# One core, a two-part network: transposes inside a chunked scan by VectorE, the scan's walk cut in thirds, and bias products taken out of two projections

## What is computed

```python
z = jax.nn.gelu(h @ w_in + b_in, approximate=False)
u, v = jnp.split(z, 2, axis=-1)
v = layernorm(v, ln_g, ln_b, LN_EPS)
v = v.reshape(bsz, n // CHUNK, CHUNK, GMLP_GROUPS, GMLP_GROUP_CH)
v = jnp.einsum('gpq,bcqgd->bcpgd', w_s, v) + b_s.T[:, :, None]
return (u * v.reshape(bsz, n, GMLP_WIDTH)) @ w_out + b_out
```

## Time and profile before

| | us |
|---|---|
| median of 3 runs | 5302.05 (5282.6 to 5308.4) |
| the profiled execution | 5314.02 |
| its span, first to last instruction | 5312.1 |
| TensorE busy in it | 3985.8 |
| stage gmi, its v half | about 2071 to 2261 |
| stage gmo | about 2330 to 2486 |
| the scan, heads 0 to 15 and the last walk | about 3690 to 4485 |

### The profile page before, as it was taken

One profiled execution on the slowest core, in us unless ns is written; L12 is line 12 of the kernel. 1 busy time (PEld: TensorE's weight loads), 2 busy tenths in 40 slices (PEclk: granted clock), 3 DMA queues, 4 the chain that ended last, 5 costly groups with the idle time before them and its releaser, 6 DMA issues. The chain is left out here.

```text
span 5312.1 us, 89186 instructions
## 1 busy us (share of the span) xinstructions
PE 3985.8 (75%) x34888; PEld 2795.1 (53%) x34888; DVE 2115.7 (40%) x4471; ACT 1349.1 (25%) x2720; POOL 1215.1 (23%) x899
## 2 busy tenths in 40 slices
PE   7755898767599869977487773876999996347784
PEld 6434676544477657664322221753888886322221
DVE  3433764435476433253200004642666663510002
ACT  2222331222333132110111111113555543111111
POOL 4101343310143424342100001421333332300000
PEclk9756899876899989888698897988999997759887
DMA  3211453222255311113399994344221222349997
GB/s 117 71 46 56 166 174 100 76 69 55 70 183 174 90 57 57 36 61 138 123 421 422 422 422 189 111 129 145 52 57 44 52 57 63 118 178 418 420 420 284
DMA packets 349502, 842.25 MB, mean 159 GB/s; under 512 B 126089, under 2 KB 191453, under 8 KB 289406
## 3 DMA queue, kind: packets, MB, share of 16 engines
q1 hardware_dynamic: 340630, 808.97, 42.4%
q0 software_dynamic: 8560, 28.85, 1.5%
HBM read 744.79 MB, written 92.93 MB: 158 GB/s over the span
## 5 line engine op out<-in xcount | busy, mean ns | idle before, releaser
L1123 DVE SCALAR_TENSOR_TENSOR f_ada<-first_hT,condition,f_ada 128x256 f32 (+1 forms) x672 | 287.1, 499 | 0.0
L2566 DVE TENSOR_TENSOR scan_R<-scan_R,scan_bank 128x256 f32<-128x256 f32 x240 | 100.9, 420 | 231.4 <-PE scan_bank L2589 229.8
L1885 PE MATMUL moe0e_p_g<-moe_ring,moe0e_xT 128*64 128x512 f32 x608 | 174.3, 653 | 17.9 <-issue 9.2
L342 POOL TENSOR_TENSOR gmi_w_lo<-gmi_w,gmi_w_hi 128x512 fp32r<-128x512 f32 x64 | 122.2, 1910 | 239.1 <-ACT gmi_w_hi L361 239.1
L2340 POOL TENSOR_TENSOR scan_off<-scan_pairs,scan_join 128x256 f32<-128x256 f32 x240 | 174.3, 765 | 0.0
L1885 PE MATMUL moe0e_p_u<-moe_ring,moe0e_xT 128*64 128x512 f32 x608 | 167.7, 631 | 0.0
L2589 PE MATMUL scan_bank<-scan_R,scan_Z 64*64 64x64 f32 x3840 | 155.1, 219 | 10.3 <-DVE scan_R L2566 9.7
L2589 PE MATMUL scan_bank<-scan_T,scan_off 64*64 64x64 f32 x3840 | 157.2, 220 | 5.6 <-issue 0.6
L1885 PE MATMUL moe1e_p_g<-moe_ring,moe1e_xT 128*64 128x512 f32 x512 | 148.2, 660 | 15.1 <-issue 8.3
L342 POOL TENSOR_TENSOR p_w_lo<-p_w,p_w_hi 128x512 fp32r<-128x512 f32 (+3 forms) x88 | 112.8, 1283 | 176.9 <-ACT p_w_hi L361 176.9
L1904 PE MATMUL moe0e_p_y<-moe_ring,moe0e_gatedT 128*64 128x512 f32 x608 | 142.8, 624 | 13.0 <-ACT moe0e_gatedT L1929 13.0
(11 more groups left out here) (707 smaller groups left out, 10659.3 us busy)
## 6 DMA issues: line engine op xcount, KB each, us to landing
moe_ring<-in_moe_w_gu_dram SPq DMA_DIRECT2D x280, 1024.0 KB, 21.9
moe_ring<-in_moe_w_down_dram SPq DMA_DIRECT2D x140, 1024.0 KB, 22.5
first_hT<-in_ada_w_dram SPq DMA_DIRECT2D x48, 1024.0 KB, 7.3
f0u_w<-in_ffn_w_gate_up_dram SPq DMA_DIRECT2D x22, 1024.0 KB, 4.9
f1u_w<-in_ffn_w_gate_up_dram SPq DMA_DIRECT2D x22, 1024.0 KB, 4.9
gmi_w<-in_ga_w_in_dram SPq DMA_DIRECT2D x64, 256.0 KB, 2.7
p_w<-in_ab_w_in_dram SPq DMA_DIRECT2D x48, 256.0 KB, 2.7
f0d_w<-in_ffn_w_down_dram SPq DMA_DIRECT2D x44, 256.0 KB, 2.7
```

The lines of the kernel that those rows point to most:

```text
L342: nc.gpsimd.tensor_tensor(w_lo[t % 2][:, 0:width], w[t % RAW][:, 0:width], w_hi[t % 2][:, 0:width], ALU.subtract).then_inc(w_lo_made, 1)
L1123: ins = nc.vector.scalar_tensor_tensor(out=dst, in0=src, scalar=cond[:, k, which:which + 1], in1=dst, op0=ALU.mult, op1=ALU.add)
L1885: mm = nc.tensor.matmul(p[r, :], xT[:, kd, r], ring[:, s, half, k, g * HID:(g + 1) * HID], start=(kd == 0), stop=(kd == KD - 1), skip_grou ...
L2566: V.tensor_tensor(R[u][:, g4, :], R[u][:, g4, :], quad(zr_bank), ALU.add).then_inc(s["zr_added"], 1)
```

## The change

In the scan:

- T comes from VectorE: after each addition into R (and after the identity is added) VectorE waits for its own write and transposes the 128x256 tile in 32x32 blocks. The twelve grown turns and the three root turns by TensorE go, and with them ScalarE's 15 copies of T. After the last level, which joins the 32-wide blocks, T is not made.
- The walk's steps 3 to 11 are cut in thirds: each slot has two thirds, one before its Z times R product and one after it, so that they fill slots 0 to 13. The product of r with the state moves from `walk_state` to `walk_solve`.
- See and the copy of y move from VectorE to ScalarE, and t1 (one 128x768 instruction per head) too.
- The bonus sums move from the start of the front part to behind `walk_state` of step 2. The sums of squares move from slot 2 to slot 5.
- b and k are turned into one bank per group and copied by three ScalarE instructions of 128x512 instead of six of 128x256. Z times R has two banks in turn, so its wait is for the addition two slots back.
- SyncE loads sg on its own, earlier; the other six transfers stay at the start of a head.

In the gated MLP:

- The bias products go. For v, VectorE adds a bias row, which is now loaded on all 128 partitions, and ScalarE does the Gelu in place, SBUF to SBUF, in steps 2 and 3 of the next job.
- For the output, GpSimd makes bias times gate (two instructions of 128x1024, in steps 1 and 2) and adds it to the six x tiles (128x1024 each, steps 3 to 8) behind its own subtractions.

```diff
@@ project_split
-                        mm = nc.tensor.matmul(view(g), l_lo[:, a:a + aw], r_hi[:, b0:b0 + bw], start=False, stop=(last and bias is None))
-                        if last and bias is not None:
-                            mm = nc.tensor.matmul(view(g), const["ones"][0:1, 0:aw], bias, start=False, stop=True)
+                        mm = nc.tensor.matmul(view(g), l_lo[:, a:a + aw], r_hi[:, b0:b0 + bw], start=False, stop=last)
...
+                    if aside:
+                        aside(pool, t)
...
+                    if jobs[c].get("post"):
+                        nc.scalar.wait_ge(dve_done, nth[g])
+                        jobs[c]["post"](groups[g][1]).then_inc(posted, 1)
@@ gmlp
-            brow = mem2.enter_context(nc.sbuf_tensor("gm_brow", [1, W_GMLP], F32))
+            brow = mem2.enter_context(nc.sbuf_tensor("gm_brow", [P, W_GMLP], F32))
...
-                    return engine.activation(v[:, j, c * BANK:(c + 1) * BANK], ps, ACT.Gelu)
+                    cols = slice(c * BANK, (c + 1) * BANK)
+                    return engine.tensor_tensor(v[:, j, cols], ps, brow[:, cols], ALU.add)
...
+                    return nc.scalar.activation(v[:, j, cols], v[:, j, cols], ACT.Gelu)
...
+            if 1 <= t <= 2:
+                nc.gpsimd.tensor_tensor(gated_bias[t - 1][:], brow[:], gates[t - 1][:], ALU.mult).then_inc(bias_gated, 1)
+            if 3 <= t < 3 + NA:
+                j = t - 3
+                pool.wait_ge(bias_gated, 2)
+                nc.gpsimd.tensor_tensor(tiles[j], tiles[j], gated_bias[j >= NT][:], ALU.add).then_inc(bias_added, 1)
@@ rwkv_scan
-    WALK_GROWTH = {n: NG + n for n in range(STEPS - NG)}
+    WALK_PARTS = [(what, j) for j in range(NG, STEPS) for what in range(3)] + [(0, STEPS)]
...
@@ rwkv_scan, ScalarE
+                def walk_x(w, j):
+                    if j > CSTEPS:
+                        n = j - 1 - CSTEPS
+                        act.wait_ge(s["y_ready"], w * lat + n + 1)
...
+                        A(yo[:, n, :], y_psum, ACT.Copy).then_inc(s["y_copied"], 1)
+                    if j < STEPS:
+                        act.wait_ge(s["x_ready"], w * STEPS + j + 1)
+                        A(X[:], x_psum, ACT.Copy).then_inc(s["x_copied"], 1)
+                    if 1 <= j < STEPS - 1:
+                        act.wait_ge(s["sm_ready"], w * STEPS + j + 1)
+                        A(See[:], Sm[:], ACT.Identity, scale=ee[w % 2][:, j:j + 1]).then_inc(s["step_made"], 1)
...
+                    if slot == 2:
+                        if h:
+                            act.wait_ge(s["km_made"], h)
+                        A(t1[:], aa[:], ACT.Identity, scale=cols(h, 1), bias=oneminus[:, h:h + 1]).then_inc(s["t1_made"], 1)
...
@@ rwkv_scan, VectorE
+                    def turn(g):
+                        g4 = slice(4 * g, 4 * g + 4)
+                        V.transpose(T[:, g4, :].rearrange("p c t -> p (c t)"), R[u][:, g4, :].rearrange("p c t -> p (c t)")).then_inc(s["t_made"], 1)
...
+                        walk_part(2 * n)
                         dve.wait_ge(s["zr_ready"], h * NZ + n + 1)
-                        V.tensor_tensor(R[u][:, g4, :], R[u][:, g4, :], quad(zr_bank), ALU.add).then_inc(s["zr_added"], 1)
-                        if walk is not None and n in WALK_GROWTH:
-                            walk_step(walk, WALK_GROWTH[n])
+                        V.tensor_tensor(R[u][:, g4, :], R[u][:, g4, :], quad(zr_bank[n % 2]), ALU.add).then_inc(s["zr_added"], 1)
+                        if l < LEVELS - 1:
+                            dve.wait_ge(s["zr_added"], h * NZ + n + 1)
+                            turn(g)
+                        walk_part(2 * n + 1)
...
@@ rwkv_scan, TensorE
                     for n in range(NZ):
...
-                        part(walk_state, j)
-                        if 1 <= n <= NZ - NG:
-                            turn_grown(n - 1)
-                        part(walk_solve, j)
+                        walk_part(2 * n)
                         pe.wait_ge(s["z_copied"], h * NZ + n + 1)
-                        if n >= 1:
-                            pe.wait_ge(s["zr_added"], h * NZ + n)
+                        if n >= 2:
+                            pe.wait_ge(s["zr_added"], h * NZ + n - 1)
                         for q in range(4):
-                            mm = mmul(zr_bank[:, q * CH:(q + 1) * CH], Z[n % 2][:, q, :], R[u][:, 4 * g + q, :])
+                            mm = mmul(zr_bank[n % 2][:, q * CH:(q + 1) * CH], Z[n % 2][:, q, :], R[u][:, 4 * g + q, :])
                         mm.then_inc(s["zr_ready"], 1)
-                        part(walk_share, j)
+                        walk_part(2 * n + 1)
```

More of the change, by code:

```diff
@@ L363, in _ @@
                         ends("act", act, nc.scalar, chain, act_done, c - 1, k)
+                    if c and 2 <= k < 4:
+                        posts(c - 1, k - 2)
                 for half in range(2):
                     ends("act", act, nc.scalar, chain, act_done, len(jobs) - 1, half)
+                    posts(len(jobs) - 1, half)
             @block.vector
@@ L2088, in gmlp @@
             s = slice(c * W, (c + 1) * W)
-            jobs.append(dict(w=a["ga_w_out_2"][:, s], mode="T", eng="dve", bias=brow[0:1, s],
-                             epi=gated_residual(lambda j, s=s: tiles[j][:, s], lambda j, s=s: gates[j >= NT][:, s], tmp)))
-        project_split(nc, "gmo", uT, ALL, jobs, const={"ones": S.ones})
+            jobs.append(dict(w=a["ga_w_out_2"][:, s], mode="T", eng="dve",
+                             epi=after_bias(gated_residual(lambda j, s=s: tiles[j][:, s], lambda j, s=s: gates[j >= NT][:, s], tmp))))
+        project_split(nc, "gmo", uT, ALL, jobs, aside=add_bias)
 def second_block_a(nc, S, a, x_tiles, c_tiles, hT, mods):
@@ L2357, in walk_sa, with walk_part @@
                     A(SA[:], sa_psum, ACT.Identity, scale=w[w_ % 3][:, j:j + 1]).then_inc(s["sa_copied"], 1)
+                def walk_part(w, p):
+                    if w is not None and p < len(WALK_PARTS):
+                        what, j = WALK_PARTS[p]
+                        if what < 2:
+                            (walk_x, walk_sa)[what](w, j)
                 def exps(*of):
@@ L2430, in _ @@
                 act.wait_ge(s["const_loaded"], 80)
+                act.wait_ge(s["consts_made"], 2)
                 for slot in range(SLOTS):
@@ L2536, in step, with walk_part @@
                             walk_step(walk, j)
+                    def walk_part(p):
+                        if walk is not None and p < len(WALK_PARTS) and WALK_PARTS[p][0] == 2:
+                            walk_step(walk, WALK_PARTS[p][1])
                     mask(0)
@@ L2638, in part, with walk_part, bonus @@
                             what(walk, j)
-                    pe.wait_ge(s["bd_ready"], h + 1)
-                    pe.wait_ge(s["kh_made"], h + 1)
-                    if h:
-                        pe.wait_ge(s["bon_read"], h)
-                    for n in range(lat):
-                        mm = mmul(bon_psum[:, n:n + 1], rk[:, n, :], S.ones[:, 0:1])
-                    mm.then_inc(s["bon_ready"], 1)
+                    def walk_part(p):
+                        if walk is not None and p < len(WALK_PARTS):
+                            what, j = WALK_PARTS[p]
+                            if j < STEPS:
+                                (walk_state, walk_solve, walk_share)[what](walk, j)
+                    def bonus():
+                        pe.wait_ge(s["bd_ready"], h + 1)
+                        if h:
+                            pe.wait_ge(s["bon_read"], h)
+                        if h >= 2:
+                            pe.wait_ge(s["y_copied"], (h - 1) * lat)
+                        for n in range(lat):
+                            mm = mmul(bon_psum[:, n:n + 1], rk[:, n, :], S.ones[:, 0:1])
+                        mm.then_inc(s["bon_ready"], 1)
+                    pe.wait_ge(s["at_ready"], h + 1)
+                    pe.wait_ge(s["kh_made"], h + 1)
                     def pair_set(i):
```

181 lines of the change are left out of this document (81 added, 100 removed).

## The result

The changed kernel takes **5147.11 us** (median of 4 runs, 5133.53 to 5157.69) against 5305.23 before (median of 4, 5282.6 to 5308.49): ratio 0.971, 95% interval 0.967 to 0.975. That is 158 us less by the medians, 135 to 173 by the interval. Forecast: 5190, range 5125 to 5250. The profiled execution took 5133.53 us, under its median.

A forecast was written before the change was run, and what follows sets the result against it. Stages run one after another; TensorE bounds the gated MLP, slowed by bias products and clock, and its written-out order bounds the scan. Terms -53.8 (v half), -8.4 (output product), -48 (fifteen heads), -2 (head 0's factors) took 5302 to 5190 us, range 5125 to 5250.

The forecast's parts named there:

- The output product: Gated MLP's output stage: 145.3 us instead of 155.7, -10.4; with the wider row load -8.4, bounds -14 and -2.
- I take 6: Output product: GpSimd's additions and subtractions, stretched by VectorE's splits, overrun steps 1 to 8, costing 6 us.
- 0.9 us for a bank: Output product: at the turn of the jobs TensorE waits 0.9 us for a bank.
- The loop: Scan, the 14 slots after slot 0's addition: 29.7 us against 31.87, -2.2 per head, bounds -5.6 and +1.
- (3): Scan loop: GpSimd's km starts at slot 2 instead of 6, beside VectorE's scan, costing 0.6 us.
- the list of slots: Scan loop: lengths laid out slot by slot, from 1.7 us for slot 0 to 1.6 for the last, summing to 27.7.
- (2): Scan loop: ScalarE's 0.84 us piece between the copies of X and SA delays `walk_share` about 0.7 us; 1.4 in all.
- Head 0: Scan, loop of head 0: no walk, TensorE working about half of it, so half clock and no gain.
- Rival A: Scan: waits go with the products; loop loses 5.6 us and front part 1.5 per head; 5132 us, chance 0.17.
- B: Scan gains nothing, from transposes of 0.69 us or more or thirds waiting in queues; 5240 us, chance 0.2.
- D: Gated MLP: bias edit doesn't restore the clock, or GpSimd's additions hold up gmo by 20 us; 5217 us, chance 0.05.
- C: Scan: the clock falls to half as TensorE's busy share drops; slower than before, 5570 us, chance 0.04.

The follow-up runs named there:

- experiment 3: The kernel before, with the bias product of v made from 128 rows instead of one: 5276.72 us, ratio 0.993 to the kernel before.
- experiment 12: The changed kernel with sums of squares spread, km late, and GpSimd's six gated-bias additions in every second output-product step: 5115.82 us, 0.964 of the kernel before.
- the version without such stretches: The changed kernel with the sums of squares spread over slots 2, 3, 4, 7 and t1, so km, two slots later: 5118.0 us.
- experiments 7: The changed kernel with ScalarE's t1, and so GpSimd's km, two slots later: 5140.0 us, ratio 0.968 to the kernel before.
- 8: The changed kernel with Sm made ahead of VectorE's transpose: 5168.53 us, ratio 0.973 to the kernel before.
- 10: The changed kernel with the sums of squares made 12 at a time behind slots 2, 3, 4 and 7: 5143.92 us, 0.969 of the kernel before.

## Why the prediction was right, and where its sum was short

The direction and the range held. The order of the parts did not: the gated MLP was to give 62 us and the scan 50, and alone they gave 77 and 84. Step by step:

- **The v half** (58.4 us for products and clock): 58.2, and the added row load 3.1 where 3.8 was said. The method, a clean step of 4.08 us times 32, needed no model of the clock, and experiment 3 shows why it had to be taken whole: about half of it was clock.
- **The output product** (-10.4): -12.6. Two terms were mis-sized, in opposite ways. GpSimd's, "I take 6", came to 3.1, in a row of steps of up to 4.64; experiment 12 got 2.7 of it back. The lengthening was right (3.11 for the addition, where the row has 2.48 without it and 0.67 was to come on top), but the subtractions between grew shorter, 1.60 in place of 1.93. The turn of the jobs, "0.9 us for a bank", cost 2.8: three steps of 6.46, 4.42 and 4.20 in place of 4.08, with the longest wait in TensorE's timeline:

```profile
2337.38 0.50 PE L326 MATMUL gmo_bank<-gmo_w_hi,gmo_x_hi 128*128 128x512 f32 x1 [1.82 <-DVE x L1489]
```

  The tail, counted from the start of the last product, was 5.1 us, within the 5.5.
- **The transposes** (0.42 + 0.07): 0.445 us each, starting 0.45 after the addition:

```profile
L2573 DVE STREAM_TRANSPOSE scan_T<-scan_R x240: 445/445/449, 3607.6 to 4277.0; 128x256 f32<-128x256 f32 x120
```

- **The loop** (-2.2 per head) **is the step whose sum was off**: -3.5 in typical heads, 28.3 us where 29.7 was said. (3), km beside VectorE, was priced at 0.6 from two scans that differ by 0.58; it cost 1.4 in slot 3, since it met not a scan but the piece behind it, and the walk's Sm stood behind that. The mis-sized term is the rest, the list of slots (27.7) with (2) (1.4): 29.1 was said and 26.9 measured. (2), ScalarE's piece ahead of SA, did come about: behind the three places named TensorE waits 0.46, 0.53 and 0.77 us for SA, and the slots of the last two took 2.18 and 2.38 where the list has 1.7. But in head 15, which has no pieces, they took 2.08 and 1.97, so its price can't be told apart from the list's. The list itself was too long in many slots: slots 0, 7, 9 and 13 took 1.33, 1.71, 1.91 and 0.94 where 1.7, 2.0, 2.25 and 1.6 stood.
- **The front part** (-1.0): -1.6.
- **Head 0** ("I expect half clock there, no gain"): wrong. Its loop kept the full clock but for 3.4 us and gained 2.1. The last walk was the wrong row to compare with: it did stay at half clock.
- **Up to the first addition of head 0** (-2): -6.8. What gave the other 5 was not tried.
- Rival A, that all waits go with the products, would have been -106 for the fifteen heads; they gave -77.7. TensorE's extra 3.1 us of idle time per head is what was given back. In time the kernel came nearer to A's 5132 than to the 5190 forecast. B falls with the transposes' 0.445 and the scan's 84 us. D falls with PEclk 1.00 in the v half and the 3.1 us of GpSimd's additions.
- **C came true on a small scale.** Heads 0 to 15 of the changed kernel have six stretches at half clock, 34 us in all of some 670 (before: three, 10 us of some 750), and two heads that take 47.1 us instead of 42.8 each hold one of 10.2 us. One begins at 3743.1, 0.5 us after the end of slot 3's wait of 1.66 us. The point from which it would have decided, a third of the heads' time, was far off, but it was worth more than the forecast gave it in a sum whose other steps are 1 us: the version without such stretches is 36.6 us faster, in part by that: its mean head is 2.4 us shorter, a head without half clock 1.9.

The prediction weighed the port rule of the Trainium skill (SBUF — State Buffer, Who interferes with whom) for the output product, where full turns would have made 8 us of GpSimd's 6 and 3.1 were measured, and did not work it out for km. By that rule VectorE's piece, started 0.3 us behind km, would wait until km ends at 3831.47 and then take its 0.95, to 3832.4. It ended at 3832.29: the trace agrees.

## What to carry to other kernels

When an instruction moves in time on GpSimd, look up which two-input VectorE instruction it will now lie beside, and who stands behind that one; here this cost 1.4 us of 42.8 and one slot number mended it, once the run of one-column products had gone from the place it was moved to. Removing work from TensorE pays only where no chain of another kind fills the slot: a turned group of 0.47 us, made by VectorE in its place, gave 0.03 where a whole walk step stood and 0.46 to 0.69 in slots with nothing but the growth. Try two changes apart and together when one opens room for the other: here each alone gave 0.6 or 1.1 us in the loop and both 3.7. Price a product of one row by what a clean step takes, not by its own length, since it may take the clock with it.

## What the runs showed of the hardware

- A float32 bias product of one row (48 records of 512 columns beside 576 others) left the v half at a granted clock of 0.84; the same product from 128 rows left it at 1.00 with 37.4 us less. At full clock one product took 1.27 us from one row and 0.87 from 128. The number of columns, and the engine's busy share (189.00 of 189.00 us, 156.79 of 157.00), were the same.
- In the scan the granted clock fell for 3.4, 6.8 or 10.2 us at a time. In heads 1 to 15 of the changed kernel and of experiments 7, 8 and 10 that happened 34 times, each time inside or shortly behind a wait of TensorE for Sm of 1.47 to 2.11 us, or behind a wait of 0.48 to 0.89 us with 48 or 32 one-column products after it. The same waits and products stood in other heads without it. With the sums spread and km late it held at 1.00 through heads whose TensorE was busy about 90% (548.78 of 611.00).
- VectorE's float32 block transpose of 128x256 takes 0.445 us, its twin right behind another 0.402.
- VectorE's piece with two SBUF inputs took 0.92 us alone and 2.33 beside GpSimd's km; GpSimd's addition took 3.11 where it lay beside both of VectorE's splits and 2.40 where it met only the start of one; VectorE's cast took 0.56 us without it and 2.51 beside it.
